# Routing two heads ahead of the experts in a two-layer kernel with gathered experts

## The reference

```
q = (h @ wq)  -> [token, 8 heads, 2 halves, 128]
s = q . keys  -> 128 scores for each head and half
top_s, top_i = top_k(s, 16)                  # for both halves
cand = top_s[half 0] + top_s[half 1]         # 16 x 16 sums
best_s, best_pos = top_k(cand, 16)           # 16 experts for each head
idx  = expert numbers;  gate = softmax(best_s)
act  = gelu(h . u_tab[idx])
out  = sum over heads and experts of gate * act * v_tab[idx]
```

## Time and profile before

| | us |
|---|---|
| median of 3 runs | 2195.55 |
| lowest, highest | 2194.63, 2203.05 |
| profiled execution | 2196.84 |
| its span | 2195.0 |
| busy in the span: PE, DVE | 1816.2, 1466.8 |
| busy in the span: ACT, POOL | 897.5, 618.9 |
| experts of layer 0, first dot to last dot | 730.0 to 1412.8 |
| experts of layer 1, first dot to last dot | 1509.1 to 2179.6 |

### The profile page before, as it was taken

The page is one execution under the profiler, slowest core; times in us unless marked ns, Lnnn a source line. Parts: engine busy times, 40 slices in busy tenths (PEclk is TensorE's granted clock), DMA queues, the critical chain, the costliest instruction groups (busy, mean ns, idle before and its releaser), DMA issues.

```text
span 2195.0 us, 21985 instructions
## 1 busy us (share of the span) xinstructions
PE 1816.2 (83%) x7101; PEld 1091.2 (50%) x7101; DVE 1466.8 (67%) x3029; ACT 897.5 (41%) x2357; POOL 618.9 (28%) x567
## 2 busy tenths in 40 slices
PE   4888999889978688888678787996798888877786
PEld 3757998788867344443323233354344443333222
DVE  6766956857776666767567767516666668677754
ACT  3446433524463333434334445312433344344433
POOL 1160000000000344434244343103354345443441
PEclk9889989989998899999899999998999899999999
DMA  9654758545563799999899999746899999999996
GB/s 367 265 198 145 262 196 306 177 171 211 202 220 116 316 371 418 418 421 421 338 402 421 421 421 421 319 172 256 362 416 419 419 421 421 421 421 421 421 422 251
DMA packets 114690, 723.76 MB, mean 330 GB/s; under 512 B 11504, under 2 KB 13344, under 8 KB 34064
## 3 DMA queue, kind: packets, MB, share of 16 engines
q0 software_dynamic: 74864, 540.30, 59.6%
q1 hardware_dynamic: 39712, 182.07, 22.7%
HBM read 721.24 MB, written 1.08 MB: 329 GB/s over the span
## 4 chain that ended last, share of the span: by engine, by line
PE 36%; DMA 31%; DVE 20%; ACT 6%; issue 5%; POOL 2%; SPq 0%; DVEq 0%; ACTq 0%; POOLq 0%
DMA X<-in_k_uv,EI 15%; PE PS L2129 14%; DMA Z<-in_k_uv,EI 9%; DMA W<-in_peer_wq 5%; PE PS L2106 5%; DVE junk L1809 4%; PE PS L1822 3%; PE PS L1823 3%; PE PS L1824 3%; DVE ACC L1429 3%; DVE WL L1445 3%; PE PS L1915 2%; ACT WH L999 1%; DMA W<-in_ada_w 1%; PE PS L2182 1%
## 5 line engine op out<-in xcount | busy, mean ns | idle before, releaser
L2129 PE MATMUL PS<-X,dg 128*128 128x512 f32 x1372 | 673.1, 626 | 176.2 <-ACT dg L999 175.4
L1809 DVE CUSTOM_DVE_ANT_0 junk<-H,X 128x1024 f32<-128x1024 f32 x343 | 419.6, 1223 | 254.0 <-DMA X<-in_k_uv,EI 247.0
L990 POOL DMA_INDIRECT X<-in_k_uv,EI x343 | 376.1, 1097 | 623.2 <-PE PS L2129 328.8
L2129 PEld LDWEIGHTS PS<-X,dg 128*128 128x128 f32 x1372 | 251.2, 195 | 553.3 <-ACT dg L999 345.6
L999 ACT ACTIVATE CF<-DOT 128x1 f32<-128x1 f32 x512 | 102.3, 200 | 588.7 <-DVE DOT L1809 588.2
L2129 PE MATMUL PS<-Z,dg 128*128 128x512 f32 x504 | 246.7, 622 | 38.3 <-ACT dg L999 38.2
L1809 DVE CUSTOM_DVE_ANT_0 junk<-H,Z 128x1024 f32<-128x1024 f32 x126 | 154.1, 1223 | 89.9 <-DMA Z<-in_k_uv,EI 86.7
L999 ACT ACTIVATE dg<-CP,CG 128x128 f32<-128x128 f32 x512 | 205.5, 401 | 17.3 <-PE PS L2129 0.6
L2129 PEld LDWEIGHTS PS<-Z,dg 128*128 128x128 f32 x504 | 92.6, 195 | 175.3 <-ACT dg L999 100.4
L1822 PE MATMUL PS<-XH,WH 128*128 128x256 f32 x592 | 176.2, 298 | 2.3 <-ACT XH L999 1.2
L990 POOL DMA_INDIRECT Z<-in_k_uv,EI x126 | 136.3, 1082 | 136.5 <-PE PS L2129 115.8
(11 more groups left out here) (312 smaller groups left out, 2626.8 us busy)
## 6 DMA issues: line engine op xcount, KB each, us to landing
W<-in_ada_w SPq DMA_DIRECT2D x56, 1024.0 KB, 5.1
Y<-in_ada_w SPq DMA_DIRECT2D x16, 1024.0 KB, 5.9
W<-in_k_win SPq DMA_DIRECT2D x16, 1024.0 KB, 5.1
W<-in_peer_wq SPq DMA_DIRECT2D x16, 1024.0 KB, 16.6
W<-in_k_ffi SPq DMA_DIRECT2D x13, 1024.0 KB, 5.4
Y<-in_k_ffi SPq DMA_DIRECT2D x9, 1024.0 KB, 4.9
W<-in_ffn_w_out SPq DMA_DIRECT2D x8, 1024.0 KB, 5.7
W<-in_ab_w_out SPq DMA_DIRECT2D x6, 1024.0 KB, 5.1
```

Source lines behind the costliest of these rows:

```text
L990: e.indirect_dma_start(out=WS[k][:, :], out_offset=None, in_=I[f"k_uv{ly}"][:, :], in_offset=bass.IndirectOffsetOnAxis(ap=EI[t][:, j:j + 1 ...
L1809: e.tensor_tensor_reduce(junk, H[:, t, :], d[:, 0:D], 1.0, 0.0, ALU.mult, ALU.add, DOT[:, j:j + 1]).then_inc(v_dot, 1)
L2129: p = e.matmul(PS[:, 2 * t + q, :], dgb[n % 4][:, :], d[:, D + q * 512:D + (q + 1) * 512], start=(j == 0), stop=(j == 127))
```

## The change

Tile 0's heads 0 and 1 are both routed in key part 0, ahead of the first expert; `h` of tile 0 stands between the two routings, `h` of tile 1 behind them. The key columns of part 0 are placed among the routing steps of head 0 (second column half, chunk 2) and behind it (chunk 3). Experts start when both `h` steps are written, with all of part 0 behind them. `others` leaves head 1 out of part 0. In layer 0, tile 0, every fourth expert is followed by a second filler step. An assertion states that the list of the expert 13 further on is in the plan.

```diff
-        if s4 == 0:
-            for lo in (0, 128):
-                for i in range(2):
-                    yield from chunk(i, lo, lo + 128)
-                if lo == 0:
-                    h00 = route(ly, 0, 0)
-                    next(h00)
-                    P("tt", ly, 1)
-                    yield from h00
-                    P("h", ly, 0)
-                    P("h", ly, 1)
-                    ready.add((ly, "h"))
-        else:
+        if s4:
             for i in range(2):
                 yield from chunk(i, 0, 256)
             yield from route(ly, 0, 2 * s4)
-        for i in range(2, 4):
-            yield from chunk(i, 0, 256)
+            for i in range(2, 4):
+                yield from chunk(i, 0, 256)
+            yield
+            return
+
+        first, second = route(ly, 0, 0), route(ly, 0, 1)
+        for i in range(2):
+            yield from chunk(i, 0, 128)
+        next(first)
+        P("tt", ly, 1)
+        next(first)
+        for i in range(2):
+            yield from chunk(i, 128, 256)
+            next(first)
+        yield from chunk(2, 0, 256)
+        yield from first
+        yield from chunk(3, 0, 256)
+        P("h", ly, 0)
+        yield from second
+        P("h", ly, 1)
+        ready.add((ly, "h"))
         yield
...
     def others(ly):
         for s4 in range(4):
             yield from keys_part(ly, s4)
-            yield from route(ly, 0, 2 * s4 + 1)
+            if s4:
+                yield from route(ly, 0, 2 * s4 + 1)
...
         for j in range(128):
             while (ly, t, j // 16) not in ready:
                 next(g)
+            ahead = 128 * t + j + 13
+            assert ahead > 255 or (ly, ahead // 128, ahead % 128 // 16) in ready, (ly, t, j)
             n = 256 * ly + 128 * t + j
             P("ga", n)
             P("dot", n)
             P("tail", n)
             next(g, None)
+            if ly == 0 and t == 0 and j % 4 == 3:
+                next(g, None)
...
         g = others(ly)
-        while not {(ly, 0, 0), (ly, "h")} <= ready:
+        while (ly, "h") not in ready:
             next(g)
```

## The result

The changed kernel took 2219.66 us (median; 2216.54 to 2225.73), the kernel before 2195.55 in the same runs. The ratio is 1.0099, 95% interval 1.0074 to 1.0123: 1% slower. Forecast were 2188 us and a range that ends at 2204.

What follows compares the result with a forecast made beforehand. The gather stream at 421 GB/s was taken as the bound. The profiled 2196.8 us less 4.3 in layer 0 and 3.0 in layer 1 gave 2189.5, or 2188 against the median; range 2170 to 2204.

Steps and rivals of the forecast that it cites:

- The bound: From 723 us to the end the gather stream is the clock, 2.49 us per expert at 421 GB/s.
- the lists: Late routed lists at gathers in both layers: removing them is worth up to 27.6 us.
- the later first dot: Start of each layer's experts: dot 0 comes 11 us later in layer 0, 15.3 in layer 1.
- the tile boundary: Between tiles 0 and 1 of layer 0: low-rate windows of 10.8 and 2.6 us are saved.
- the consumers run out of reserve in layer 0: Key parts of layer 0: reserve gone by about gather 40, then consumers bound; DMA share under 1 about 840 to 950 us.
- my 13.4: Layer 0 behind its key parts: the 10.8 and 2.6 us saved at the tile boundary, set against 9.1 lost.
- the key parts of layer 0: Tails 0 to 65 take 199.5 us, 3.0 each; at gather 77 layer 0 is 9.1 us behind.
- the slabs: ldq slabs 2 and 3, 2 x 2.5 us, come early beside the first 12 gathers; no wait for them counted.
- the dips that I allowed for: PE dropping to its lower clock level in route phases: half a microsecond a phase pair, +3 us, bounds 0 and 14.
- layer 1: Whole layer ends 3.0 us earlier, with the 7.5 of its old low-rate window already in it.
- the limit of 24.2: Ring of 12 gathers: for an unbroken stream tail n may end at most 24.2 us after gather n landed.
- Rival B: Slower: consumers past the reserve, PE's clock falling in each cycle, both layers 10.8 us later, 2210 us; chance 0.08.

Runs made afterwards that it cites:

- e2: The kernel before with a second filler step behind each expert from 99 on in layer 0, tile 0, nothing else; 2188.54 us, ratio 0.9964.
- e10: e6 with no extra filler step while a head's routing is in progress, made up for as soon as it is done; 2197.78 us, ratio 1.0001.
- e9: The changed kernel with every expert's dot product over 512 of its 1024 columns; 2209.19 us, ratio 1.0051.
- e4: The changed kernel with only the first of two column halves of each tail's products, except at a tile's first expert; 2199.64 us, ratio 1.0011.
- e3: The kernel before with part 0's key columns ahead of the experts, head 1 routed right behind the first, late extra steps from expert 96; 2178.44 us.
- e5: The changed kernel with eight empty filler steps ahead of key part 1 in both layers, its slabs issued as before, no assertion; 2207.91 us, ratio 1.0041.
- e1: The changed kernel without the second filler step on every fourth expert of layer 0, tile 0, and without the assertion; 2196.66 us, ratio 0.9999.
- e6: e3 with the changed kernel's second filler step on every fourth expert of layer 0, tile 0 as well; 2204.38 us, ratio 1.0040.
- e11: e3 without its late extra steps behind experts 96 to 127 of layer 0; 2176.04 us, ratio 0.9903.

## Why the prediction was wrong

**Right.** The bound (the gather stream), the lists (12 waits became 3), the later first dot (19.5 us behind the first gather against forecasts of 17.8 and 21.9), the tile boundary, whose windows are full now, and that the consumers run out of reserve in layer 0. Where they do I had wrong: the rate is low from about 760 to 970, for the 840 to 950 that I gave, since the reserve is gone at gather 14 and not at 40. The 13.0 us from dot 127 (30.1 behind before's) to dot 255 (17.1) are close to my 13.4 in part by luck: the lag of the dots is in them, and the same count gives 24.4 in e2, where the layer gained 7.9.

**The first term that failed: the key parts of layer 0**, "so at that point layer 0 is 9.1 us behind". From tail 0 on PE to the end of tail 65 I had 204.2 us (743.3 to 947.5, with 3 us of clock dips in it). Gather 77 is issued as tail 65 ends, at 960.35, and tail 0 begins at 740.35: 220.0. Of the 15.8 us more, 6.0 are the two slab waits. I costed the slabs at nothing, with "the ldq slabs 2 and 3 (2 x 2.5 us) now come early beside them". They are issued early and land late, and tails stand behind the columns that wait for them. My rows for the pace of a key part had no slab wait in them. The score products show the rest cycle by cycle:

```profile
767.18 0.61 PE L2130 MATMUL PS<-KK,PQ 128*128 128x128 f32 x4
800.19 0.61 PE L2130 MATMUL PS<-KK,PQ 128*128 128x128 f32 x4
836.68 0.61 PE L2130 MATMUL PS<-KK,PQ 128*128 128x128 f32 x4
871.61 0.61 PE L2130 MATMUL PS<-KK,PQ 128*128 128x128 f32 x4
905.62 0.61 PE L2130 MATMUL PS<-KK,PQ 128*128 128x128 f32 x4
940.69 0.61 PE L2130 MATMUL PS<-KK,PQ 128*128 128x128 f32 x4
```

From tail 0 to the first of them it is 26.8 us, where I had 17.2 and 1.75 for the low clock: 4.7 of the 7.9 more are the slab wait, and 3.2 PE's lower level over more of its records, 1.7 of them in the 3.57 us behind the wait. The five cycles are 173.5 us where my count of steps, without dips, gives 165.0 (199.5 less that first 17.2 and the last routing phase, 17.3): 1.35 of the 8.5 are a slab wait, the other 7.2 are doubled pieces and what I could not separate. The last routing phase is 19.7 for 17.3. These make 18.8, and the dips that I allowed for cover 3.0 of them. e10 puts the doubled pieces at 7.4 us in layer 0. At gather 77 the layer is then 19.1 us behind the forecast (251.0 for 231.9): the 15.8, 1.6 of a later first tail, and 1.7 because its landing took 9.3 us, with gather 76 still ahead of it and a load of 512 KB (in_ln_g, issued at 961.43) beside it. From 970 on the stream is full, and only 2.2 us more are lost up to dot 255.

**The second: layer 1**, forecast 3.0 earlier, measured 6.0 later. I had let the reserve hold from a start near 20 us under the limit of 24.2, with no wait between the first tails. The slab wait of 6.62 us at 1552.06 is what I put at nothing, and here too gather 14 is the first that comes too late (issued 29.1 us behind the landing of gather 2). The slab waits in the layer make 8.97 us, 5.9 more than before's 3.08. But they are not a cost by themselves: e9 keeps them at 9.04 us and e4 has 11.9, and both end the layer within 1 us of e3. VectorE or PE has less to do there and can catch up, which is my reading. e5 gives the columns room instead and gives 13.3 back. That is 7.3 us under the kernel before, nearly the whole 7.5 of the old dip; the 4.5 that I had taken off it for late consumers at the end of the key parts don't show there. So layer 1 loses by late dot, key columns and slab wait together, past the ring's reserve, and how its 12.0 us over e3 are shared isn't shown.

**What the sum did not ask.** Packing was costed as a tail pace of 3.0 us for each of 65 experts, with the ring's reserve against it, but not compared with the same kernel without it. e1 and e6 do: 22 and 25 us. Nothing pays that back, because behind the key parts the stream already runs at 2.49 us per expert and can't go faster when the other engines have less to do. The gain of packing, the boundary, was to be had for 7.9 us in e2 without packed key parts, and in e11 by an earlier routing with no extra step.

Rival B had the right side and the right resource, consumers past their reserve, with the wrong carrier: clock dips in both layers at 21.6 us, where packing, its doubled pieces among it, and in both layers the late start with slab waits were the price. I gave it 0.08 because I took my own cycle count, made of rows without slab waits and without doubled pieces, as good to half a microsecond a cycle.

Left open: how much of the packed stretch's price is PE's clock and how much the turns of PE and DVE (e4 and e9 changed both), and what the slab wait costs by itself.

## What to carry to other kernels

Where one stream of transfers is the clock, spread the other engines' work so that each transfer has no more than its own time beside it. Finishing that work sooner gives nothing back, and bunching it costs where the other engines already need nearly a transfer's time, as in the key parts here; doubled steps behind experts 96 to 127 cost nothing. A load issued while a ring of gathers fills may land behind gathers issued after it (28.3 us here): issue it ahead of them, or place what needs it further back, and look at what is queued behind the waiting instruction. When a list must be ready ahead, ask when the ring would run dry, not when the slot comes free; at the tile boundary 4 experts were enough. The best version with the right output is e11_no_late (2176.0; e3 is its equal by the intervals): it puts all key columns of part 0 ahead of the experts, so that head 1's routing starts with the first of them, and drops the rest.

## What the runs showed of the hardware

The second of two slabs of 1 MiB issued together on the hardware queue took 25.5 to 29.0 us in the five links of the chain above, whether it was issued in the middle of the first twelve indirect gathers of the software queue (725.08) or into their steady stream (797.36). The first of the pair took 16.8 us at both places. The shortest gather took 5.5.

Taking work away from PE lowered its clock. With half of each tail the mean granted clock of the span went from 0.939 to 0.788, and in the stretch above PE stayed busy 142.4 us for 349 matmul records where it had been 172.9 for 472: 408 ns for each record instead of 366, though fewer of them were the long ones of the tails.

The DMA share isn't the rate. It was 0.89 at 290 GB/s from 790 to 800, and 0.99 at 386 from 1550 to 1570, both with the ring short of gathers. Read the two columns together.
